# Latent attention in a two-layer block: gate pieces in two halves around the turned weights, and another order of their reading

## The chip, the cores and the metric

The kernel runs on one core of a Trainium2 chip. The metric is device time in microseconds (us) of one launch, median of three runs. Engines are named as in the profile: PE is TensorE (PEld its weight loads), DVE is VectorE, ACT is ScalarE, POOL is GpSimd, SP is SyncE.

## The reference

512 tokens pass a first block (sparse and dilated attention, then a mixture of experts) and two further layers. The change lies in the attention routine that both parts share. The two stages that matter:

```
# first block: three attentions over 8 heads, mixed by gates
o = gb[..., 0:1] * o_c + gb[..., 1:2] * o_s + gb[..., 2:3] * o_w
gm = jax.nn.sigmoid(mg)                       # merge gates, 16 pieces of 128 rows
# each of the two further layers: latent attention over 8 heads
sc = jnp.einsum('bqhd,bkhd->bhqk', q_blk, k) * scale
sc = jnp.where(qpos[:, None] >= kpos[None, :], sc, jnp.finfo(jnp.float32).min)
p = jax.nn.softmax(sc, axis=-1)
o = jnp.einsum('bhqk,bkhe->bqhe', p, v)
gates = jax.nn.sigmoid(gate_logits)           # (h @ w_in), 24 pieces of 128 rows
```

## The kernel before

`paired_attention` (L202) does all three attention stages. Work goes in **units**: one pair of heads (sides u = 0, 1) and one block of 128 queries. The latent stage (`mla`, called once in each of the two layers) has 16 units: four pairs of heads times t = 0 to 3, where unit n has t = n mod 4 and sees (t + 1) x 128 keys. The stage `nsa` of the first block has 16 units too, `dil` has 8. The order on each engine is written out by hand, and semaphores alone join the engines.

The steps of a unit, by the names of the code:

- `score(n)` on PE (L259, masks L263): products of queries and keys into PSUM.
- `largest(n)` on DVE (L337, L338), `exps(n)` on ACT (L394).
- `weigh(n)`: the weights of side 0 are scaled on DVE (L348, L359); in `mla` those of side 1 are scaled on ACT (L414).
- `turn(n, c)` on PE (L278): transposes of the weights, in chunks of up to two key blocks (one chunk for t = 0 and 1, two for t = 2 and 3). `copy(n, c)` (L368) brings a chunk from PSUM to SBUF, in `mla` always on DVE.
- `mix(n, c)` on PE (L294): value products from the copied chunk. `store(n)` on ACT (L408).

`AHEAD` is the number of score buffers: 2 in `mla`, 1 in `nsa` and `dil`. Beside the attention PE computes **gate pieces**: 24 matmuls of 128x512 each (`Gates.tensor`, L2800 to L2802 through `three`). In `mla` 11 of the 16 units have one, those in `GATE_PAIRS` = (0, 1, 2, 3, 5, 7, 9, 11, 13, 14, 15), called gated below; units 4, 6, 8, 10 and 12 have none. In `nsa` every unit has one. All gate pieces of these stages go through a single PSUM bank: the first matmul of the next piece waits until DVE has read the last one (`take`, L1269). The split of a later weight piece into two parts (`high` on ACT L562, `low` on DVE L570) goes along with each gated unit, and SP loads the pieces ahead.

The order before, for unit n of `mla`: PE does the last `mix` of unit n - 1, the whole gate piece, `score(n + 2)`, then waits for the scaled weights, and does `turn` with the next `mix` right behind it. DVE does `weigh(n)`, `largest(n + 1)`, `low`, the copies, `take(n)`. ACT does its part of `weigh(n)`, `store(n - 1)`, `exps(n + 1)`, `high`. With `lead` true (`mla` and `nsa`) the first gate piece stands ahead of the loop.

Of the kernel before, what the change touches and what calls it, by code (L numbers as in the profile page):

```python
# [26 lines left out]
P = 128  # L27
# [3 lines left out]
DC = D // P  # L31
# [170 lines left out]
def paired_attention(nc, name, C, pairs, scale, cols, places, beside, by_scalar, lead):  # L202
# [4 lines left out]
    N, SIDES, WIDE, RING = len(pairs), 2, 4 * P, 3  # L207
# [4 lines left out]
    AHEAD = len(scores_at)  # L212
    two_engines = AHEAD == 2
    with Stage(nc, name) as st:
# [25 lines left out]
        with st.block() as block:  # L240
# [9 lines left out]
            @block.tensor  # L250
            def _(pe):
                def score(n):
                    scores = scores_at[n % AHEAD]
                    if n >= AHEAD:
                        pe.wait_ge(exp_done, SIDES * (n - AHEAD + 1))
                    for bank, parts, width in pairs[n].products:
                        for j, (q, keys) in enumerate(parts):
                            for u in range(SIDES):
                                nc.tensor.matmul(scores[:, u, bank:bank + width], q[u], keys[u], start=(j == 0), stop=False)  # L259
                        for after, at, mask in pairs[n].masks:  # L260
                            if after == bank:
                                for u in range(SIDES):
                                    mm = nc.tensor.matmul(scores[:, u, at:at + mask.shape[1]], C.mask_ident, mask, start=False, stop=True)  # L263
                    mm.then_inc(scored, 1)

                def turn(n, c):
                    g = before[n] + c
                    if g >= 2:
                        pe.wait_ge(*copied_after(g - 2))
                    if c < extra:  # L270
                        of = pairs[n].extra[0]
                        mm = nc.tensor.transpose(turned[g % 2][0:of.shape[1], 0:P], of, C.ident[:, :])
                    else:
                        blocks = blocks_of(n, c)
                        for u in range(SIDES):
                            for j, (col, _) in enumerate(blocks):
                                at = (u * len(blocks) + j) * P
                                mm = nc.tensor.transpose(turned[g % 2][:, at:at + P], probs[n % 2][:, u, col:col + P], C.ident[:, :])  # L278
                    mm.then_inc(turn_done, 1)

                def mix(n, c):
                    g = before[n] + c
                    pe.wait_ge(*copied_after(g))
                    if c == 0 and n >= 1:
                        pe.wait_ge(stored, n)
                    if c < extra:
                        v = pairs[n].extra[1]
                        mm = nc.tensor.matmul(mixed, v, probs_t[g % RING][0:v.shape[0], 0:P], start=True, stop=False)
                    else:
                        blocks = blocks_of(n, c)  # L290
                        for j, (_, v) in enumerate(blocks):
                            for u in range(SIDES):
                                rows, at = slice(64 * u, 64 * u + 64), (u * len(blocks) + j) * P
                                mm = nc.tensor.matmul(mixed[rows, :], v[:, rows], probs_t[g % RING][:, at:at + P],  # L294
                                                      start=(c == 0 and j == 0), stop=(c == chunks[n] - 1 and j == len(blocks) - 1))
                    mm.then_inc(chunk_mixed, 1)

                for n in range(AHEAD):
                    score(n)
                if lead:  # L300
                    beside.tensor(pe, 0)
                else:
                    idle_products(nc, C, turned[0], 10)
                for n in range(N):
                    if AHEAD == 1 and n + 1 < N:
                        score(n + 1)
                    if n >= 1:
                        mix(n - 1, chunks[n - 1] - 1)
                    if n >= 1 or not lead:
                        beside.tensor(pe, n)  # L310
                    if AHEAD == 2 and n + 2 < N:
                        score(n + 2)
                    for c in range(chunks[n]):
                        if c == extra:
                            pe.wait_ge(scaled, by_vector * (n + 1))
                            if two_engines:
                                pe.wait_ge(scaled_s, n + 1)
                        turn(n, c)
                        if c >= 1:
                            mix(n, c - 1)  # L320
                mix(N - 1, chunks[N - 1] - 1)
                idle_products(nc, C, turned[0], 8)

            @block.vector
            def _(dve):
# [14 lines left out]
                def weigh(n):  # L340
                    if n >= 2:
                        dve.wait_ge(scaled, by_vector * (n - 1))
                        if two_engines:
                            dve.wait_ge(scaled_s, n - 1)
                    for u in range(SIDES):
                        at = SIDES * n + u + 1
                        dve.wait_ge(exp_done, at)
                        V.reciprocal(rden[n % 2][:, u, :], den[n % 2][:, u, :]).then_inc(inverted, 1)  # L348
                        if u >= by_vector:
                            continue  # L350
                        dve.wait_ge(inverted, at)
                        if weighted:
                            V.tensor_tensor(wgt[n % 2][:, u, :], rden[n % 2][:, u, :], pairs[n].weights[:, u, :],
                                            ALU.mult).then_inc(weights_done, 1)
                            dve.wait_ge(weights_done, at)
                        by = wgt[n % 2]
                        for k, (col, width) in enumerate(pairs[n].parts):
                            pr = probs[n % 2][:, u, col:col + width]
                            ins = V.tensor_scalar(pr, pr, by[:, u, k:k + 1], None, ALU.mult)  # L359
                        ins.then_inc(scaled, 1)  # L360
# [9 lines left out]
                largest(0)  # L370
                for n in range(N):
                    weigh(n)
                    if AHEAD == 1:
                        beside.vector(dve, n)
                    if n + 1 < N:
                        largest(n + 1)
                    if AHEAD == 2:
                        beside.vector(dve, n)
                    for c in range(by_scalar, chunks[n]):
                        copy(n, c)  # L380
                    beside.after(dve, n)

            @block.scalar
            def _(act):
# [55 lines left out]
class CompressedWeights:  # L440
# [24 lines left out]
    def tensor(self, pe, n):  # L465
        if n not in self.FIRST:
            return
        h = self.FIRST.index(n)
        if h >= 1:
            pe.wait_ge(self.shift_done, h)  # L470
        for j in range(2):
            for t in range(TT):
                at = (TT * j + t) * 2 * N_CMP
                out = self.bank[:, at:at + 2 * N_CMP].rearrange("p (u c) -> p u c", u=2)
                self.nc.tensor.matmul(out, self.z[:, Z_Q + 2 * h + j, t * P:(t + 1) * P], self.k_both, start=True, stop=False)
                add = self.masks[:, t * N_CMP:(t + 1) * N_CMP].unsqueeze(1).to_broadcast([P, 2, N_CMP])
                mm = self.nc.tensor.matmul(out, self.ident, add, start=False, stop=True)
        mm.then_inc(self.scored, 1)
# [700 lines left out]
class Angles:  # L1179
# [42 lines left out]
    def turn(self, act, j):  # L1222
        act.wait_ge(self.reduced, j + 1)
        to = (self.C.sin2, self.C.cos2)[j]
        self.nc.scalar.activation(to[self.rows, :], self.left[j][self.rows, :], ACT.Sin)


class Gates:
# [40 lines left out]
        self.nc.vector.tensor_tensor(self.m[:, s, :], self.place(c)[0], self.x_rstd,  # L1269
                                     ALU.mult).then_inc(self.taken, 1)  # L1270

    def tensor(self, pe, c):
        bank, last = self.place(c)
        if last >= 0:
            pe.wait_ge(self.taken, last + 1)
        hi, lo = self.stream.ready(pe, self.at(c))
        for k, at in enumerate(slices(DC)):
            mm = three(self.nc, bank, hi[:, at], lo[:, at], self.x_hi[:, k, :], self.x_lo[:, k, :], k == 0,
                       k == DC - 1)
        mm.then_inc(self.stream.used, 1)  # L1280


class GatesByUnit:
# [39 lines left out]
class GatesByPair(GatesByUnit):  # L1323
# [9 lines left out]
    def after(self, dve, n):  # L1333
        if n in self.slots:
            self.gates.take(dve, self.slots[n])


def pool_and_gla(nc, name, C, y, values, w_a2, w_pool, scale, m, head_root, bank, gates):
# [1473 lines left out]
def slices(n, width=P):  # L2812
    return [slice(k * width, (k + 1) * width) for k in range(n)]
# [777 lines left out]
```

## Time and profile before

| | us |
|---|---|
| median of 3 runs | 3619.53 |
| lowest, highest | 3617.75, 3620.05 |
| span of the profiled execution | 3620.0 |
| PE busy in it | 3509.2 (97%) |
| DVE busy | 2323.1 (64%) |
| ACT busy | 1428.6 (39%) |

The profile is of one execution. A row of a timeline begins with the start and the duration in us; what stands in square brackets is the idle time of that engine just before, and what ended it. The end of a PE matmul is modelled, so the idle time of PE is a little shorter than what the next instruction has waited, and the idle time of its weight loads (PEld) is also shown. PEclk is the granted TensorE clock: 1.00 is 2.4 GHz, 0.50 is 1.2 GHz.

### The profile page before, as it was taken

The page shows a single profiled execution, that of the slowest core. Times are in us where ns is not written, and L with a number is a line of the kernel's source. Part 1 is how long each engine was busy: PE and PEld are TensorE (multiplying, and loading weights), DVE is VectorE, ACT ScalarE, POOL GpSimd, SP SyncE. Part 2 cuts the span into 40 slices and gives each one's busy share as a digit, 9 for nine tenths or more (in the row PEclk, how much of TensorE's full clock was granted, in tenths as well). Part 3 has the DMA queues.
Part 4 walks back from the last instruction along what each step waited for, and adds up shares of the span by engine and source line. Part 5 has one row for each costly group of instructions (what it writes and reads, how often), then busy time and mean ns, then how long its engine had stood idle before and what let it go on. Part 6 is the DMA issues. An engine that isn't in the chain of part 4 may idle for free. (4 is left out here: it accounts for less than half of the span.)

```text
span 3620.0 us, 47480 instructions
## 1 busy us (share of the span) xinstructions
PE 3509.2 (97%) x18217; PEld 2997.8 (83%) x18224; DVE 2323.1 (64%) x4211; ACT 1428.6 (39%) x2390; POOL 377.4 (10%) x280
## 2 busy tenths in 40 slices
PE   8999999999999899999999999999999999999998
PEld 6776778999999899999887767788878776778887
DVE  6656766889999798888635546544343544655433
ACT  4343343433899443333323234433232323443221
POOL 1000000000233336434100000000000000000000
PEclk9999999999999999999999999999999999999999
DMA  4321243555899999999522224232322222423332
GB/s 148 102 65 50 65 142 100 202 168 168 306 364 367 370 367 396 388 377 389 204 94 82 77 70 152 79 107 97 93 88 93 82 75 73 145 85 105 99 92 71
DMA packets 213172, 597.38 MB, mean 165 GB/s; under 512 B 22258, under 2 KB 80404, under 8 KB 211412
## 3 DMA queue, kind: packets, MB, share of 16 engines
q1 hardware_dynamic: 176084, 460.13, 38.1%
q0 software_dynamic: 36864, 134.23, 9.6%
q8 instruction: 145, 2.38, 0.3%
q14 instruction: 79, 0.65, 0.1%
HBM read 523.36 MB, written 69.21 MB: 164 GB/s over the span
## 5 line engine op out<-in xcount | busy, mean ns | idle before, releaser
L562 ACT ACTIVATE stream_hi<-stream_raw 128x1024 fp32r<-128x1024 f32 (+1 forms) x611 | 638.9, 1046 | 1060.3 <-PE ffn_ps L2802 416.9
L570 DVE TENSOR_TENSOR stream_lo<-stream_raw,stream_hi 128x1024 fp32r<-128x1024 f32 (+1 forms) x611 | 740.3, 1212 | 442.2 <-ACT stream_hi L562 439.6
L1140 PE MATMUL experts_ps<-mix_a_hi,stream_hi 128*128 128x384 f32 x1024 | 342.9, 335 | 15.4 <-issue 15.4
L598 PE MATMUL experts_ps<-h_hi,stream_hi 128*128 128x384 f32 x1024 | 346.7, 339 | 1.1 <-PEq L728 1.1
L1140 PE MATMUL experts_ps<-mix_a_lo,stream_hi 128*128 128x384 f32 x1024 | 342.8, 335 | 0.0
L1140 PE MATMUL experts_ps<-mix_a_hi,stream_lo 128*128 128x384 f32 x1024 | 342.7, 335 | 0.0
L598 PE MATMUL experts_ps<-h_lo,stream_hi 128*128 128x384 f32 x1024 | 342.2, 334 | 0.0
L598 PE MATMUL experts_ps<-h_hi,stream_lo 128*128 128x384 f32 x1024 | 342.2, 334 | 0.0
L2800 PE MATMUL mid_ps<-h_hi,stream_hi 128*128 128x512 f32 x672 | 280.3, 417 | 4.1 <-PEq L3030 2.2
L2800 PE MATMUL ffn_ps<-h_hi,stream_hi 128*128 128x512 f32 x704 | 280.7, 399 | 2.7 <-DVE h_lo L2856 2.7
L2802 PE MATMUL ffn_ps<-h_hi,stream_lo 128*128 128x512 f32 x704 | 274.0, 389 | 0.0
L2801 PE MATMUL ffn_ps<-h_lo,stream_hi 128*128 128x512 f32 x704 | 274.0, 389 | 0.0
L2801 PE MATMUL mid_ps<-h_lo,stream_hi 128*128 128x512 f32 x672 | 264.8, 394 | 0.0
L2802 PE MATMUL mid_ps<-h_hi,stream_lo 128*128 128x512 f32 x672 | 264.4, 393 | 0.0
L662 POOL DMA_INDIRECT experts_rows<-u_rows,experts_slot_at x128 | 160.4, 1253 | 622.9 <-DVE experts_rows L672 476.3
L662 POOL DMA_INDIRECT experts_rows<-v,experts_slot_at x128 | 195.7, 1529 | 217.8 <-DVE mix_sums L690 188.7
L1140 PEld LDWEIGHTS experts_ps<-mix_a_hi,stream_hi 128*128 128x128 f32 x1024 | 192.8, 188 | 15.7 <-issue 15.7
L598 PEld LDWEIGHTS experts_ps<-h_hi,stream_hi 128*128 128x128 f32 x1024 | 192.4, 188 | 1.8 <-issue 1.4
L1140 PEld LDWEIGHTS experts_ps<-mix_a_lo,stream_hi 128*128 128x128 f32 x1024 | 192.8, 188 | 0.0
L1140 PEld LDWEIGHTS experts_ps<-mix_a_hi,stream_lo 128*128 128x128 f32 x1024 | 192.8, 188 | 0.0
L598 PEld LDWEIGHTS experts_ps<-h_lo,stream_hi 128*128 128x128 f32 x1024 | 192.5, 188 | 0.0
L598 PEld LDWEIGHTS experts_ps<-h_hi,stream_lo 128*128 128x128 f32 x1024 | 192.2, 188 | 0.0
(510 smaller groups left out, 6840.3 us busy)
## 6 DMA issues: line engine op xcount, KB each, us to landing
stream_raw<-u SPq DMA_DIRECT2D x128, 512.0 KB, 3.9
stream_raw<-v SPq DMA_DIRECT2D x128, 512.0 KB, 8.2
stream_raw<-l_gu SPq DMA_DIRECT2D x88, 512.0 KB, 3.3
expert_hidden<-experts_gelu SPq DMA_DIRECT2D x128, 192.0 KB, 4.1
expert_weights<-built SPq DMA_DIRECT2D x12, 2048.0 KB, 10.6
built<-expert_weights SPq DMA_DIRECT2D x16, 1536.0 KB, 13.9
stream_raw<-l_gate SPq DMA_DIRECT2D x48, 512.0 KB, 3.9
built<-expert_hidden SPq DMA_DIRECT2D x124, 192.0 KB, 8.7
```

The lines of the kernel that those rows point to most:

```text
L562: self.nc.scalar.activation(self.hi[n % self.RING][:, 0:w], self.raw[n % self.RAW][:, 0:w], ACT.Copy).then_inc(self.hi_done, 1)
L570: self.nc.vector.tensor_tensor(self.lo[n % self.RING][:, 0:w], self.raw[n % self.RAW][:, 0:w], self.hi[n % self.RING][:, 0:w].bitcast(F32) ...
L598: mm = self.nc.tensor.matmul(self.ps[n % 2], a, b[:, k, :], start=(k == 0 and m == 0), stop=(k == DC - 1 and m == 2))
L662: self.nc.gpsimd.indirect_dma_start(self.rows[n % self.RING][:, :], None, source, bass.IndirectOffsetOnAxis(ap=self.at[:, j:j + 1], axis=0 ...
L1140: mm = nc.tensor.matmul(out[d][:, DIRECT:SEQ], v, a[b % RING][:, :], start=(b == 0 and m == 0), stop=(b == KEYS - 1 and m == 2))
L2800: nc.tensor.matmul(out, hi, x_hi, start=first, stop=False)
L2801: nc.tensor.matmul(out, hi, x_lo, start=False, stop=False)
L2802: return nc.tensor.matmul(out, lo, x_hi, start=False, stop=last)
```

## The change

In `mla` (`AHEAD` 2) PE has another order. For a gated unit: `score(n + 2)`, first half of the gate piece (12 matmuls), the wait for the scaled weights, all of `turn(n)`, second half of the gate piece, all of `mix(n)`. For a unit without a gate piece: the wait, `turn(n)`, `score(n + 2)`, `mix(n)`. Unit 0 is gated but has its `score(2)` behind `turn(0)`. On DVE `take(n - 1)` moves from behind the copies of unit n - 1 to behind `weigh(n)`, in front of `largest(n + 1)`. ACT, SP and POOL keep their order.

For `AHEAD` 1 the order stays, with one difference: the gate piece that `lead` had put ahead of the loop now stands in the loop, so that in `nsa` it comes behind `score(1)`.

```
                 for n in range(AHEAD):
                     score(n)
-                if lead:
-                    beside.tensor(pe, 0)
-                else:
+                if not lead:
                     idle_products(nc, C, turned[0], 10)
                 for n in range(N):
-                    if AHEAD == 1 and n + 1 < N:
-                        score(n + 1)
-                    if n >= 1:
-                        mix(n - 1, chunks[n - 1] - 1)
-                    if n >= 1 or not lead:
+                    if AHEAD == 1:
+                        if n + 1 < N:
+                            score(n + 1)
+                        if n >= 1:
+                            mix(n - 1, chunks[n - 1] - 1)
                         beside.tensor(pe, n)
-                    if AHEAD == 2 and n + 2 < N:
+                        for c in range(chunks[n]):
+                            if c == extra:
+                                scaled_by_both(n)
+                            turn(n, c)
+                            if c >= 1:
+                                mix(n, c - 1)
+                        continue
+                    gated = n in beside.slots
+                    if gated and n >= 1 and n + 2 < N:
                         score(n + 2)
+                    beside.half(pe, n, 0)
+                    scaled_by_both(n)
                     for c in range(chunks[n]):
                         turn(n, c)
-                        if c >= 1:
-                            mix(n, c - 1)
-                mix(N - 1, chunks[N - 1] - 1)
+                    if (not gated or n == 0) and n + 2 < N:
+                        score(n + 2)
+                    beside.half(pe, n, 1)
+                    for c in range(chunks[n]):
+                        mix(n, c)
+                if AHEAD == 1:
+                    mix(N - 1, chunks[N - 1] - 1)
...
                     weigh(n)
+                    if AHEAD == 2 and n >= 1:
+                        beside.after(dve, n - 1)
...
-                    beside.after(dve, n)
+                    if AHEAD == 1:
+                        beside.after(dve, n)
+                if AHEAD == 2:
+                    beside.after(dve, N - 1)
...
-    def tensor(self, pe, c):
+    def tensor(self, pe, c, rows=range(DC)):
         bank, last = self.place(c)
-        if last >= 0:
+        if rows[0] == 0 and last >= 0:
             pe.wait_ge(self.taken, last + 1)
...
+    def half(self, pe, n, which):
+        if n in self.slots:
+            self.gates.tensor(pe, self.slots[n], range(which * DC // 2, (which + 1) * DC // 2))
```

PE, first `mla` stage, around the turned weights of unit 1 (a gated one; `stream_const,mla_probs` is `turn`, `mla_probs_t,v` is `mix`, `k,q` and `stream_masks` are `score`, `h_hi` and `h_lo` the gate piece). Before:

```order
L2802 MATMUL mid_ps<-h_hi,stream_lo 128x512
L259 MATMUL mid_ps<-k,q 128x512 x4
L263 MATMUL mid_ps<-stream_masks 128x128 x2
L278 MATMUL mid_ps<-stream_const,mla_probs 128x128 x4
L294 MATMUL mid_ps<-mla_probs_t,v 64x128 x4
L2800 MATMUL mid_ps<-h_hi,stream_hi 128x512
```

`mix` stood right behind `turn`, and the gate piece behind `mix`. Now the turned weights of unit 3 (the line numbers of the gate piece are 24 higher in the changed file):

```order
L2826 MATMUL mid_ps<-h_hi,stream_lo 128x512
L2824 MATMUL mid_ps<-h_hi,stream_hi 128x512
L2825 MATMUL mid_ps<-h_lo,stream_hi 128x512
L2826 MATMUL mid_ps<-h_hi,stream_lo 128x512
L278 MATMUL mid_ps<-stream_const,mla_probs 128x128 x8
L2824 MATMUL mid_ps<-h_hi,stream_hi 128x512
L2825 MATMUL mid_ps<-h_lo,stream_hi 128x512
L2826 MATMUL mid_ps<-h_hi,stream_lo 128x512
```

`turn` has gate matmuls on both sides; `mix` has moved behind twelve of them.

The same engine at unit 4, which has no gate piece, before:

```order
L259 MATMUL mid_ps<-k,q 128x384 x4
L263 MATMUL mid_ps<-stream_masks 128x128 x2
L278 MATMUL mid_ps<-stream_const,mla_probs 128x128 x2
L294 MATMUL mid_ps<-mla_probs_t,v 64x128 x2
L2800 MATMUL mid_ps<-h_hi,stream_hi 128x512
```

And now:

```order
L278 MATMUL mid_ps<-stream_const,mla_probs 128x128 x2
L259 MATMUL mid_ps<-k,q 128x384 x4
L263 MATMUL mid_ps<-stream_masks 128x128 x2
L294 MATMUL mid_ps<-mla_probs_t,v 64x128 x2
L259 MATMUL mid_ps<-k,q 128x512 x4
L263 MATMUL mid_ps<-stream_masks 128x128 x2
L2824 MATMUL mid_ps<-h_hi,stream_hi 128x512
```

The score products of unit 6 have moved between `turn` and `mix` of unit 4, those of unit 7 ahead of the gate piece of unit 5.

PE at the start of `nsa`, before:

```order
L250 UNCONDITIONAL_BRANCH
L259 MATMUL first_ps<-z 128x128 x4
L263 MATMUL first_ps<-masks_sb 128x128 x4
L2800 MATMUL first_ps<-h_hi,stream_hi 128x512
L2801 MATMUL first_ps<-h_lo,stream_hi 128x512
```

And now:

```order
L250 UNCONDITIONAL_BRANCH
L259 MATMUL first_ps<-z 128x128 x4
L263 MATMUL first_ps<-masks_sb 128x128 x4
L259 MATMUL first_ps<-z 128x256 x4
L263 MATMUL first_ps<-masks_sb 128x128 x4
L2824 MATMUL first_ps<-h_hi,stream_hi 128x512
L2825 MATMUL first_ps<-h_lo,stream_hi 128x512
```

The score products of unit 1, which wait for the exponentials of unit 0, have moved ahead of the first gate piece.

## Rows read from the trace of the kernel before

**Rows 1.** The page: busy time of each engine, with its share of the span.

```profile
PE 3509.2 (97%) x18217; PEld 2997.8 (83%) x18224; DVE 2323.1 (64%) x4211; ACT 1428.6 (39%) x2390; POOL 377.4 (10%) x280
```

**Rows 2.** Waits of PE, whole run: line, releaser, total us, times, longest us.

```profile
PE mid_ps L294 <- DVE mla_probs_t L368: 18.0, 32, 0.8
...
PE up_ps L2800 <- DVE up_y_lo L2664: 1.9, 1, 1.9
...
PE mid_ps L278 <- issue: 0.7, 4, 0.2
```

**Rows 3.** Busy time in the two `mla` stages: us and count by engine, PEclk, DMA.

```profile
2085.00:2207.00 122.00, 112.35 (x667) 76.89 (x668) 60.42 (x159) 41.64 (x108) 0.00 (x0) 1.00 0.26 74
2991.00:3113.00 122.00, 111.96 (x666) 76.59 (x664) 60.33 (x159) 41.38 (x107) 0.00 (x0) 1.00 0.27 76
```

**Rows 4.** Who waited for the copied chunks, by tile: total us, times.

```profile
  PEld mid_ps L294: 27.0, 40
```

**Rows 5.** Timeline of the first `mla` stage: weight loads behind `turn`, and one hand-over.

```profile
2105.75 0.42 PEld L294 LDWEIGHTS mid_ps<-mla_probs_t,v 128*64 128x64 f32 x8 [1.02 <-DVE mla_probs_t L368]
...
2114.38 0.64 PEld L294 LDWEIGHTS mid_ps<-mla_probs_t,v 128*64 128x64 f32 x12 [0.80 <-DVE mla_probs_t L368]
...
2149.95 0.42 PEld L294 LDWEIGHTS mid_ps<-mla_probs_t,v 128*64 128x64 f32 x8 [0.58 <-DVE mla_probs_t L368]
...
2153.85 0.20 PEld L294 LDWEIGHTS mid_ps<-mla_probs_t,v 128*64 128x64 f32 x4 [0.75 <-DVE mla_probs_t L368]
...
2164.13 0.72 PEld L259 LDWEIGHTS mid_ps<-k,q 64*128 64x128 f32 x8 [0.17 <-issue]
```

**Rows 6.** Timeline of the same stage, DVE and ACT, from the copy of unit 1.

```profile
2105.01 0.69 DVE L368 COPY mla_probs_t<-mid_ps 128x512 f32<-128x512 f32 x1 [3.87 <-PE mid_ps L278]
2105.62 0.68 DVE L1269 TENSOR_TENSOR m_rows<-mid_ps,x_rstd 128x512 f32<-128x512 f32 x1
...
2106.22 0.15 DVE L348 RECIPROCAL mla_rden<-mla_den 128x1 f32<-128x1 f32 x1
...
2106.82 0.67 DVE L337 TENSOR_REDUCE mla_top<-mid_ps 128x1 f32<-128x512 f32 x1
...
2108.50 0.69 ACT L394 ACTIVATE mla_probs<-mid_ps,mla_bias 128x512 f32<-128x512 f32 x1
...
2109.17 1.05 ACT L562 ACTIVATE stream_hi<-stream_raw 128x1024 fp32r<-128x1024 f32 x1
2110.26 1.23 DVE L570 TENSOR_TENSOR stream_lo<-stream_raw,stream_hi 128x1024 fp32r<-128x1024 f32 x1 [1.79 <-ACT stream_hi L562]
```

**Rows 7.** Timeline of the same stage, PE: a gate piece's start, scores, `mix`.

```profile
2096.45 0.50 PE L2800 MATMUL mid_ps<-h_hi,stream_hi 128*128 128x512 f32 x1 [0.16 <-DVE m_rows L1269]
...
2102.12 2.19 PE L259 MATMUL mid_ps<-k,q 64*128 64x512 f32 x8
...
2105.76 0.66 PE L294 MATMUL mid_ps<-mla_probs_t,v 128*64 128x128 f32 x8 [0.78 <-DVE mla_probs_t L368]
...
2164.13 0.91 PE L259 MATMUL mid_ps<-k,q 64*128 64x128 f32 x8
```

**Rows 8.** Timeline of the start of `nsa`, PE and ACT.

```profile
297.54 0.40 PE L263 MATMUL first_ps<-masks_sb 128*128 128x128 bf16 x4
...
299.93 0.22 ACT L394 ACTIVATION_READ_ACCUMULATOR nsa_probs<-first_ps,nsa_bias 128x1 f32 x1
...
303.39 1.13 PE L259 MATMUL first_ps<-z 64*128 64x256 f32 x8
...
306.82 0.48 PE L288 MATMUL first_ps<-nsa_probs_t,v_cmp 64*128 64x128 f32 x2 [1.42 <-DVE nsa_probs_t L368]
...
307.81 2.93 PE L259 MATMUL first_ps<-z 64*128 64x384 f32 x8 [0.50 <-ACT nsa_probs L394]
```

**Rows 9.** PE in two stretches: busy us (count), PEclk, DMA share, GB/s.

```profile
474.00:478.00 4.00, 4.00 (x12) 0.59 1.03 353
...
1997.00:2007.00 10.00, 10.00 (x29) 0.50 0.17 59
```

More of the change, by code:

```diff
@@ L296, in mix, with scaled_by_both @@
                     mm.then_inc(chunk_mixed, 1)
+                def scaled_by_both(n):
+                    pe.wait_ge(scaled, by_vector * (n + 1))
+                    if two_engines:
+                        pe.wait_ge(scaled_s, n + 1)
                 for n in range(AHEAD):
                     score(n)
-                if lead:
-                    beside.tensor(pe, 0)
-                else:
+                if not lead:
                     idle_products(nc, C, turned[0], 10)
                 for n in range(N):
-                    if AHEAD == 1 and n + 1 < N:
-                        score(n + 1)
-                    if n >= 1:
-                        mix(n - 1, chunks[n - 1] - 1)
-                    if n >= 1 or not lead:
-                        beside.tensor(pe, n)
-                    if AHEAD == 2 and n + 2 < N:
+                    if AHEAD == 1:
[3 more added lines that the diff above has]
+                            mix(n - 1, chunks[n - 1] - 1)
+                        beside.tensor(pe, n)
+                        for c in range(chunks[n]):
[7 more added lines that the diff above has]
+                    if gated and n >= 1 and n + 2 < N:
@@ L312, in _ @@
                         score(n + 2)
+                    beside.half(pe, n, 0)
+                    scaled_by_both(n)
                     for c in range(chunks[n]):
[L314 to L317, printed above, removed]
                         turn(n, c)
-                        if c >= 1:
-                            mix(n, c - 1)
-                mix(N - 1, chunks[N - 1] - 1)
+                    if (not gated or n == 0) and n + 2 < N:
+                        score(n + 2)
@@ L1270, in take @@
                                      ALU.mult).then_inc(self.taken, 1)
-    def tensor(self, pe, c):
+    def tensor(self, pe, c, rows=range(DC)):
         bank, last = self.place(c)
-        if last >= 0:
+        if rows[0] == 0 and last >= 0:
             pe.wait_ge(self.taken, last + 1)
         hi, lo = self.stream.ready(pe, self.at(c))
-        for k, at in enumerate(slices(DC)):
+        for k in rows:
+            at = slice(k * P, (k + 1) * P)
             mm = three(self.nc, bank, hi[:, at], lo[:, at], self.x_hi[:, k, :], self.x_lo[:, k, :], k == 0,
                        k == DC - 1)
-        mm.then_inc(self.stream.used, 1)
+        if rows[-1] == DC - 1:
+            mm.then_inc(self.stream.used, 1)
 class GatesByUnit:
```

## Prediction

> **What bounds the kernel now.** I read the page first. PE is busy 3509.2 of 3620.0 us [rows 1]: it is the bound, 111 us of idle time are all that an edit which only reorders can win, and an engine other than PE matters only where PE waits for it. So the second view is the list of PE's waits. Its longest line belongs to this stage: `mix` waits 32 times, 18.0 us, for the copy of the turned weights [rows 2]. 32 is every unit of both latent stages. The third view is the busy time in the stages: 112.35 and 111.96 of 122 us [rows 3], so some 10 us of idle time in each, nearly all of it this wait, and a granted clock of 1.00 throughout. DVE (60 us of 122) and ACT (42) have room on average; whether they have it at the right place is the question below.
>
> **What the wait is worth.** The 18.0 us are counted from the modelled end of the last transpose. The weight loads show the same wait from the side that is issued: 27.0 us, 40 times [rows 4]. By kind of unit it is 0.75 us (t = 0), 1.02 (t = 1), 0.80 (t = 2) and 0.58 (t = 3) [rows 5]. Each kind comes 8 times: 8 x 3.15 = 25.2 us; the other eight times are second chunks, (27.0 - 25.2) / 8 = 0.2 each. Not all of that is lost: where nothing is waited for, the load behind narrow products still comes 0.17 us late (the last of [rows 5]), and the 0.2 are just that. So a unit can win 0.58, 0.85, 0.63, 0.41, and all of them 25.2 - 32 x 0.17 = 19.8 us.
>
> **Part 1, gated units (22).** Between `turn` and `mix` now stand 12 gate matmuls. A whole piece takes from 2096.45 to 2102.12, 5.67 us [rows 7], a half 2.8. The copies take 0.61 us for one chunk of 512 (2105.01 to 2105.62) and twice that for two [rows 6]: 1.2 plus some 0.1 to start, under the cover of 2.8. The wait goes. If the cover were gone it would be back at its 0.41 to 0.85. The split adds one more change from narrow products to a gate piece, and takes one away (`mix` to gate becomes `mix` to `score`); I cost it at nothing, with 0 to 0.1 us x 22 = 2 us for the range.
>
> **Part 2, units without a gate piece (10).** Between `turn` and `mix` stands `score(n + 2)`. For n = 4, 8, 12 it is 384 keys wide, near 1.8 us (between the 0.91 of 128 and the 2.19 of 512 [rows 7]): cover enough. For n = 6 and 10 it is the narrow one, 0.91 and its mask, 0.97 in all, and here the move on DVE counts. Call T the end of `turn(9)`. DVE copies to T + 0.7, weighs (0.60 from 2106.22 to 2106.82 [rows 6]), then stands in front of `take(9)` until the second half piece is done at T + 2.8, and reads it in 0.6 (2105.62 to 2106.22): T + 3.5. `largest(11)` is 512 wide, 1.7 us (2106.82 to the second exponential at 2108.50 [rows 6]): T + 5.2. Only then the first copy, to T + 5.8. PE: half piece 2.8, `mix(9)` 0.6 [rows 7], `turn(10)` 0.9, score 1.0: T + 5.3. A wait of about 0.6 with the signal's way stays at units 6 and 10 of both layers, 0.7 as I take it: 4 x 0.7 = 2.8 us. Units 14 and 15 have no score left: `take` ends at T + 3.5, and the next gate piece would start at T + 2.8 + 0.6 (unit 14) or + 0.8 (unit 15). I take 0.8 us in both layers together.
>
> **Part 3, what else waits behind the moved `take`.** On DVE `largest`, `low` and the copies are queued behind it; on ACT `exps`, then `high`, for which `low` waits. From the end of a half piece the chain is: `take` 0.7, from `largest` to the second exponential 1.7, that one and `high` to 2110.26, 1.8, `low` 1.2, copy 0.6 [rows 6]: 6.0 us. PE has for it, until `mix(n)` needs the copy: `mix` 0.6, a score of 1 to 2.2, half piece 2.8, `turn` 0.6, half piece 2.8: at least 7.8. It is hidden, with 1.8 us to spare; without that it would cost PE its excess in each gated unit. SP stores a piece behind its `take`, some 3 us later than before, and a load is queued behind the store; the loads run pieces ahead of a unit of about 9 us, and I cost that at nothing. The waits that PE had apart from the copies (0.7 us in front of `turn` in 4 units [rows 2]; 0.16 for the bank of the gate pieces [rows 7], once a layer) make 1.0 us in all, and go.
>
> **Part 4, the start of `nsa`.** The diff moves a gate piece there as well. Before, it covered the exponentials of unit 0. Now PE ends `score(0)` at 297.94 and must wait for the last of them, 299.93 + 0.22 = 300.15 [rows 8]: 2.2 us idle where there was none. Behind it the two waits of 1.42 and 0.50 [rows 8] go, since the gate piece now covers weighing and `largest(1)`. Idle time alone: 2.2 - 1.9 = 0.3 us lost, but the 8 score matmuls at 307.81 took 2.93 us [rows 8] where 384 keys take about 1.8: the clock was low there. In the other place where PE sat idle that long, 1.9 us in front of the up product [rows 2], the next 4 us had a clock of 0.59 [rows 9], worth 4 x 0.41 = 1.6 us. So one low stretch goes (307.8 to about 311) and one comes (from about 301, in the gate piece). Counted through by instruction, `score(1)` 1.5, gate piece 5.7, transposes 0.7, from 300.2 with 1.7 us for the low clock: `score(2)` starts at 309.9 and ends at 311.7, where it ended at 311.07 before. I take +0.9 us; without the low stretch it is -0.8.
>
> The Trainium skill (TensorE: Matmul & The Clock Gate, "Why this matters for your kernels") warns only of gaps longer than this one; by it the low stretch would not come and the sum would be 1.7 us smaller. The trace has 1.9 us of idle time followed by a clock of 0.59, and the measurement decides. The same page ("A second HAM failure mode: psum-queue depth-cycling") says that many short idles between groups of products can themselves bring the clock down; the stage here has 32 such gaps at a clock of 1.00 [rows 3], so nothing is won back there.
>
> **Sum.** -19.8 - 1.0 + 2.8 + 0.8 + 0.9 = -16.3 us. 3620.0 - 16.3 = 3603.7 for the profiled execution; that is 0.5 above the median of the runs (3619.53), so 3603 for the median.
>
> **Rivals.**
> (a) *DVE has less room than I count.* If the 0.7 us wait also comes at units 4, 8 and 12 and half the gated units keep some 0.4, then 6 x 0.7 + 11 x 0.4 = 8.6 us stay: a gain of 8, 3611. For it: `take` now waits for PE, with everything else of DVE and ACT behind it. Against it: 1.8 us to spare.
> (b) *Slower.* The ring half piece, `take`, `largest`, `exps`, `high`, `low`, copy, `mix` becomes the bound of all 22 gated units. It decides once it is over the time that PE has, 7.8 to 9 us against the 6.0 of the rows. To eat the gain of 16.3 and lose 0.2% (7 us) beyond it, it would need 24 / 22 = 1.1 us over that in each, some 9 to 10 us in all, one and a half times its rows. At that: 3627.
> (c) *The clock.* Low stretches occur with PE fully busy too: 1997 to 2007 at 0.50 [rows 9], 5 us lost, and the like in the second layer. What I move is upstream of them; if one goes, 3598, if one more comes, 3608.
> (d) *Everything hidden*: no new waits and no low stretch in `nsa`: -19.8 - 1.0 - 0.8 = -22, 3598.
> (e) *It doesn't do what it says*: PE would find another wait of the same size in place of each, since `mix` and the next `turn` hang on the same DVE. Then 3620. The trace has DVE idle 3.87 us in front of the copy [rows 6], which speaks against it.
>
> **How the numbers follow.** Forecast (gain of 13 to 20) 0.60; (d) 0.12; (c) 0.10, half to each side; (a) 0.12; (e) 0.03; (b) 0.03. 0.2%, about what a measurement of this kernel can tell from no change, is 7.2 us: faster means below 3612.3. That holds for the forecast, (c), (d) and most of (a): 0.91; same 0.06; slower 0.03. The range: 3596 (all hidden and a low stretch less) to 3612 (rival (a)); what lies outside is (b), (e), a part of (a) and of (d).
>
> **What would show it.** Right: the wait of `mix` for the copies falls from 18.0 us to under 3; the `mla` stages take some 8.6 us less each; the rest of that wait stands at units 6 and 10; one wait of 2.2 us for `nsa_probs` at 298, and a low clock near 301 instead of 308. Wrong: PE waiting for ACT or DVE in front of `score` or `turn` in gated units (part 3, rival (b)); a gate piece waiting for its bank in many units; low stretches of the clock in other places.

## The result

| | before | changed |
|---|---|---|
| median of 4 runs on the same chip, us | 3618.66 | 3600.85 |
| lowest, highest | 3617.75, 3620.05 | 3596.70, 3602.54 |
| ratio, 95% interval | | 0.9949 [0.9937, 0.9961] |
| span of the profiled execution | 3620.0 | 3594.9 |

The kernel is 17.8 us faster, 16.5 were forecast for the median (3603). Its profiled execution is the fastest of its four and stands 25.1 us below that of before, so the two numbers have to be explained apart.

The list of PE's waits of the changed kernel (line, releaser, total us, times, longest us) answers to [rows 2]:

```profile
PE first_ps L259 <- ACT nsa_probs L412: 2.3, 1, 2.3
...
PE mid_ps L294 <- DVE mla_probs_t L381: 2.1, 4, 0.5
PE up_ps L2824 <- DVE up_y_lo L2688: 1.9, 1, 1.9
...
PE mid_ps L2824 <- DVE m_rows L1287: 0.4, 2, 0.2
```

`mix` waits 4 times instead of 32, 2.1 us instead of 18.0. The waits of 1.42 and 0.50 us at the start of `nsa` [rows 8] are gone, and 2.3 us for the exponentials have come in their place. The wait in front of `turn` (L278, 0.7 us) is gone from the list.

How long a latent stage takes is read from its first score product to the first idle product behind its last `mix`. Timeline of PE, before:

```profile
2085.05 0.91 PE L259 MATMUL mid_ps<-k,q 64*128 64x128 f32 x8 [0.44 <-PEq L1615]
...
2206.41 0.82 PE L2809 MATMUL mid_ps<-stream_masks 128*128 128x512 bf16 x3
```

and changed:

```profile
2084.52 0.91 PE L259 MATMUL mid_ps<-k,q 64*128 64x128 f32 x8 [0.44 <-PEq L1639]
...
2195.47 1.90 PE L2833 MATMUL mid_ps<-stream_masks 128*128 128x512 bf16 x8
```

That is 121.4 us before and 111.0 us now; the second layer has 121.3 and 110.9. **The two stages give 20.8 us.** The start of `nsa`, from its first score to the first value product of unit 0 (L294), took 14.2 us and takes 12.8. The remaining 2.9 us of the 25.1 (20.8 in the stages, 1.4 at the start of `nsa`) lie in code that the change doesn't touch, nearly all between the two latent stages (2206.41 to 2991.84 before, 2195.47 to 2978.03 now: 785.4 and 782.6 us). There the clock differs (PE busy us, count, PEclk, DMA share, GB/s; first before, then changed):

```profile
2870.00:2950.00 80.00, 75.38 (x333) 0.89 0.22 68
```

```profile
2870.00:2950.00 80.00, 78.06 (x339) 0.94 0.25 69
```

0.05 of 80 us is up to 4 us of full clock; 2.8 us is what the two stretches differ by. Which executions get it changes from run to run: another profiled execution of the same changed kernel (e5 below) has 0.89 there, and 785.5 us between the stages.

### The profile page after: what moved, and what is told of

It is laid out like the page before. It is cut to its first block and busy times, and to the rows that moved or that the text cites. A ratio compares the mean times of both kernels' runs of the same rounds, so it can differ in the third digit from the quotient of the medians.

```text
span 3594.9 us, 47480 instructions
## 1 busy us (share of the span) xinstructions
PE 3500.2 (97%) x18217; PEld 2993.1 (83%) x18224; DVE 2325.5 (65%) x4211; ACT 1430.5 (40%) x2390; POOL 352.1 (10%) x280
## 5 line engine op out<-in xcount | busy, mean ns | idle before, releaser
L680 POOL DMA_INDIRECT experts_rows<-v,experts_slot_at x128 | 169.4, 1324 | 243.8 <-DVE mix_sums L708 214.0
```

Source lines behind the costliest of these rows:

```text
L680: self.nc.gpsimd.indirect_dma_start(self.rows[n % self.RING][:, :], None, source, bass.IndirectOffsetOnAxis(ap=self.at[:, j:j + 1], axis=0 ...
```

## The experiments

Each kernel was run beside the kernel before on the same chip. The stage lengths and the `nsa` stretch are read from each trace as above.

| kernel | stage 1, us | stage 2, us | `nsa` start, us | median, us | before, us | ratio, 95% interval |
|---|---|---|---|---|---|---|
| before | 121.4 | 121.3 | 14.2 | | | |
| change | 111.0 | 110.9 | 12.8 | 3600.85 | 3618.66 | 0.9949 [0.9937, 0.9961] |
| e5 change again | 111.0 | 110.9 | 14.4 | 3598.90 | 3620.04 | 0.9942 [0.9929, 0.9956] |
| e1 latent stages only | 110.9 | 110.9 | 12.7 | 3597.75 | 3621.84 | 0.9939 [0.9926, 0.9953] |
| e2 `nsa` only | 121.3 | 121.3 | 14.4 | 3620.84 | 3621.84 | 1.0001 [0.9992, 1.001] |
| e3 take behind copies | 115.1 | 115.1 | 14.4 | 3607.66 | 3621.84 | 0.9964 [0.9952, 0.9976] |
| e4 score ahead of turn | 112.2 | 112.3 | 14.4 | 3603.63 | 3621.84 | 0.9956 [0.9941, 0.9971] |
| e6 piece not split | 110.7 | 113.8 | 14.4 | 3601.35 | 3620.04 | 0.9949 [0.9934, 0.9964] |
| e10 one more DVE step | 115.4 | 112.3 | 14.4 | 3605.82 | 3618.52 | 0.9968 [0.9955, 0.9981] |
| e7 three more DVE steps | 124.2 | 121.2 | 14.4 | 3622.82 | 3620.04 | 1.0009 [1.0, 1.0018] |
| e8 other pairs, `nsa` halves | 109.7 | 109.8 | 10.6 | 3593.23 | 3620.04 | 0.9923 [0.9909, 0.9936] |
| e9 the same, one split | 108.6 | 108.6 | 10.6 | 3589.72 | 3618.52 | 0.9921 [0.9908, 0.9935] |

### The two halves of the change apart

e1 has the changed latent stages, and `nsa` as before:

```
                 if not lead:
                     idle_products(nc, C, turned[0], 10)
+                elif AHEAD == 1:
+                    beside.tensor(pe, 0)
...
-                        beside.tensor(pe, n)
+                        if n >= 1 or not lead:
+                            beside.tensor(pe, n)
```

> The changed order in the two latent stages alone; the start of the nsa stage is as before (gate piece 0 ahead of score(1)). Theory: all of the gain is the copy waits that go, so each latent stage takes 111.0 us from its first score product to its last idle one's start (121.4 before), 20.8 us less in both, and the kernel is 20 us faster than before, give or take 2 us of low clock elsewhere. Rival (the prediction's part 4): the nsa part costs 0.9 us, so that this kernel is 0.9 us faster than the full change; against it the trace of the changed kernel, by which the nsa part saves 1.4 us and this one would be that much slower.

e2 is the kernel before with the new start of `nsa`:

```
-                if lead:
+                if lead and AHEAD == 2:
                     beside.tensor(pe, 0)
-                else:
+                elif not lead:
                     idle_products(nc, C, turned[0], 10)
...
-                    if n >= 1 or not lead:
+                    if n >= 1 or not lead or AHEAD == 1:
```

> Only the start of the nsa stage is changed (score(1) ahead of gate piece 0); the latent stages are as before. Prediction's part 4: PE waits 2.2 us for the exponentials, a low stretch of the clock follows near 301 and the one near 308 goes, +0.9 us from the first score of nsa to gate piece 1. Rival, by the trace of the changed kernel: no low stretch follows 2.3 us of idle time, -1.4 us over the same span. The latent stages stay at 121.4 us and the wait of mix for the copies at 18.0 us. In the total either is at the edge of what 5 rounds can tell.

e1 alone is 24.1 us faster, 2 us more than its expectation allowed; e2 alone cannot be told from the kernel before. All of the gain that the change brings is in the latent stages. What e1 shows beyond 20.8 lies elsewhere in its profiled execution: 1.5 us at the start of `nsa`, which had no low stretch of the clock this time, and 1.3 between the stages (784.1 us). e2 keeps its wait of 18.0 us, e1 has 2.1.

The length of the `nsa` start depends on the clock, and both theories had half of it. PE in four stretches of e2 (busy us, count, PEclk, DMA share, GB/s):

```profile
296.00:300.00 4.00, 1.97 (x17) 1.00 0.00 0
300.00:304.00 4.00, 3.35 (x16) 0.66 0.10 14
304.00:308.00 4.00, 4.00 (x18) 0.91 0.32 119
308.00:312.00 4.00, 4.00 (x29) 1.00 0.02 4
```

and of e1, which has the old start:

```profile
304.00:308.00 4.00, 2.08 (x19) 1.00 0.28 105
308.00:312.00 4.00, 4.00 (x28) 1.00 0.00 0
```

In e2 the clock falls behind the 2.3 us of idle time, as it does in e3 to e7 and e10; in the one profiled execution of the change that was compared first it did not. In e1 the two waits of 1.4 and 0.5 us are followed by a full clock, where the kernel before had a low stretch. So the new order takes 12.8 us without a low stretch and 14.4 with it, the old one 12.7 and 14.2. **Like with like, the `nsa` part costs 0.1 to 0.2 us.**

> The full change once more, beside the kernels of this call. Theory: 111.0 us for each latent stage, 14.4 us from the first score of nsa to the first value product of its unit 0 where a low stretch of the clock follows the 2.3 us of idle time, 12.8 where it doesn't; in the total 20 to 24 us faster than before. If the total again shows 18 us while the stages show 20.8, the rest is lost to low stretches of the clock elsewhere.

The second run of the change, on another chip, is 21.1 us faster than before, with the same stages to 0.1 us. The two intervals overlap; the stages account for 20.8.

### What on DVE and PE makes the gain

e3 leaves `take` where it was, behind the copies:

```
-                    if AHEAD == 2 and n >= 1:
-                        beside.after(dve, n - 1)
...
-                    if AHEAD == 1:
-                        beside.after(dve, n)
-                if AHEAD == 2:
-                    beside.after(dve, N - 1)
+                    beside.after(dve, n)
```

> The new order on PE, but DVE reads the gate piece where it did before, behind the copies and ahead of the next weighing. Theory: DVE then stands in front of the second half piece (2.8 us) before it weighs the next unit, so that PE waits for the scaled weights in the units without a gate piece: about 0.6 us at units 4, 8, 12 and 1.5 us at 6 and 10, in place of 0.5 at the mix of 6 and 10: each latent stage 3 to 4 us longer than with the change (114 to 115 us), the total 7 us slower than it. Rival: the place of this step does not matter since DVE is busy for half of the stage only; then 111 us and the same total.

The stages are 4.1 us longer than with the change. Its waits of PE in the latent stages are this one line:

```profile
PE mid_ps L278 <- DVE mla_probs L372: 10.2, 10, 1.5
```

Ten times, once for each unit without a gate piece, and the wait is now in front of `turn`. In the timeline of its second stage the units 4 and 6 show it as 0.7 and 1.5 us:

```profile
3024.70 0.41 PE L278 MATMUL mid_ps<-stream_const,mla_probs 128*128 128x128 f32 x2 [0.70 <-DVE mla_probs L372]
...
3037.81 0.85 PE L278 MATMUL mid_ps<-stream_const,mla_probs 128*128 128x128 f32 x6 [1.49 <-DVE mla_probs L372]
```

DVE stands in front of the second half piece before it weighs. The move of `take` is a needed part of the change: the PE order alone gives 12.5 of the 20.8 us. The other half, `take` moved in the kernel before with PE's order left alone, was not run.

e4 keeps the score products ahead of `turn` in the units without a gate piece:

```
+                    if not gated and n + 2 < N:
+                        score(n + 2)
                     beside.half(pe, n, 0)
...
-                    if (not gated or n == 0) and n + 2 < N:
+                    if n == 0:
                         score(n + 2)
```

> As the change, but in the five units without a gate piece score(n+2) stays ahead of turn, so that mix stands right behind turn there. Theory: those units keep their wait for the copy, 0.6 us at 4, 8, 12 and 0.7 to 0.8 at 6 and 10, the others have none: each stage about 2 us longer than with the change (113 us), the total 4 us slower. Rival: the score is no cover, since DVE has take and largest ahead of the copies; then 111 us.

```profile
PE mid_ps L294 <- DVE mla_probs_t L383: 5.7, 10, 0.7
```

The wait for the copy stands in all ten of those units, 5.7 us where the change has 2.1 in four of them, and the stages are 1.3 us longer (2 expected). Keeping the score ahead of `turn` costs 2.6 of the 20.8 us, an eighth of the whole.

e6 doesn't split the gate piece. Unit 0 then has nothing to cover its weighing:

```
-                    beside.half(pe, n, 0)
                     scaled_by_both(n)
...
-                    beside.half(pe, n, 1)
+                    beside.tensor(pe, n)
```

> The gate piece is not split: all 24 of its matmuls stand between turn and mix. Theory: the cover of the copy is what counts, not the split; the only new wait is at unit 0, where nothing covers the first weighing (about 1.2 us per stage), so each stage is 112 us and the total 2 us slower than with the change. Rival: the first half is needed to cover the weighing in every gated unit; then PE waits in front of turn by some 0.5 to 1 us in 11 units, each stage 5 to 10 us longer (116 to 121 us).

The first stage takes 110.7 us, less than with the split and less than the 112 expected, although PE waits 0.7 us at unit 0. The theory that the cover of the copy is what counts holds; the rival, by which every gated unit needs the first half, falls. The second stage took 113.8, and there the clock was low right behind that wait (the same wait in the first stage was followed by 1.00):

```profile
2975.00:2982.00 7.00, 6.30 (x33) 0.77 0.08 29
2982.00:2986.00 4.00, 4.00 (x12) 0.55 0.66 197
```

### How much room DVE has

e7 and e10 put k = 3 and k = 1 more DVE instructions, whose results are not used, behind `take`:

```
                     if AHEAD == 2 and n >= 1:
                         beside.after(dve, n - 1)
+                        for _ in range(k if n - 1 in beside.slots else 0):
+                            V.tensor_tensor(beside.spare[_][:, :], beside.gates.x_rstd, beside.gates.x_rstd, ALU.mult)
```

> As the change, with three more DVE instructions of 128x512 (0.6 to 0.7 us each, their results are not used) behind take in each of the 11 gated units of each stage: 2 us more on the chain take, largest, exps, high, low, copy, mix. Prediction's part 3: 1.8 us to spare there, so almost nothing in gated units and up to 2 us more at the mix of units 6 and 10: each stage 4 to 5 us longer (115 to 116). Rival (DVE has less room): by a count of every unit's rows, some 1 us more is lost at units 4, 8, 12 and 14 as well, 8 us per stage (119), and the total 16 us slower than with the change.

> As e7, with one more DVE instruction of 128x512 behind take in place of three. Theory (DVE has less room than the prediction counted only at units 6 and 10): the copy of units 6 and 10 comes 0.6 us later, 1.1 us of wait in place of 0.5, the others stay without a wait: each stage 1.3 us longer than with the change (112.3 us), the total 3 us slower, and no low stretch of the clock inside the stages. Rival: the gated units are at their limit too, 0.6 us more in each, 6 us per stage (117).

The waits of PE for the copies, first e7, then e10:

```profile
PE mid_ps L296 <- DVE mla_probs_t L383: 14.5, 12, 2.3
```

```profile
PE mid_ps L296 <- DVE mla_probs_t L383: 4.5, 4, 1.1
```

With 0.6 us more (e10) only units 6 and 10 wait, 1.1 us instead of 0.5, and the undisturbed stage is 112.3 us, as expected. With 1.9 us more (e7) the timeline of PE shows units 4 and 6 so:

```profile
3035.59 0.44 PE L296 MATMUL mid_ps<-mla_probs_t,v 128*64 128x128 f32 x4 [0.68 <-DVE mla_probs_t L383]
...
3049.15 0.88 PE L296 MATMUL mid_ps<-mla_probs_t,v 128*64 128x128 f32 x12 [2.33 <-DVE mla_probs_t L383]
```

Units 8 and 12 wait 0.7 as well, unit 10 2.3, unit 14 0.6, and unit 15 waits 0.7 for its bank; the other gated units still don't wait. The rival of e7's expectation was right on where, and 7.2 us of waits for copies per stage stand against 1.1 with the change. The queue of DVE in a unit without a gate piece, with all that stands ahead of its copy, is this (DVE, e7, unit 6):

```profile
3044.40 0.69 DVE L1291 TENSOR_TENSOR m_rows<-mid_ps,x_rstd 128x512 f32<-128x512 f32 x1 [1.48 <-PE mid_ps L2830]
3045.01 1.89 DVE L391 TENSOR_TENSOR mla_spare<-x_rstd 128x512 f32<-128x512 f32 x3
3046.81 0.69 DVE L352 TENSOR_REDUCE mla_top<-mid_ps 128x1 f32<-128x512 f32 x1
...
3048.40 1.02 DVE L383 COPY mla_probs_t<-mid_ps 128x512 f32<-128x512 f32 x2
```

What no theory had is the clock; e10's said that no low stretch would come inside the stages. The stages of e7 took 124.2 and 121.2 us where the waits alone give some 118, and one stage of e10 took 115.4 instead of 112.3. PE behind one wait of each, in e10 and in e7 (busy us, count, PEclk):

```profile
2156.00:2160.00 4.00, 4.00 (x23) 0.51 0.00 0
```

```profile
3075.00:3079.00 4.00, 3.52 (x20) 0.54 0.02 4
```

The other wait of the same 1.1 us in the same stage of e10 was followed by a full clock. In all, the low stretch came behind one of the four waits of 1.1 us (e10) and behind three of the four of 2.3 us (e7), and cost about 3 us each time.

### Two further versions

The rows of the change name what it left: 0.5 us at units 6 and 10, where the score is the narrow one, and 2.3 us at the start of `nsa`. e8 changes both:

```
-GATE_PAIRS = (0, 1, 2, 3, 5, 7, 9, 11, 13, 14, 15)
+GATE_PAIRS = (0, 1, 2, 3, 6, 7, 10, 11, 13, 14, 15)
...
                     if AHEAD == 1:
+                        if n == 0 and lead:
+                            beside.half(pe, 0, 0)
                         if n + 1 < N:
                             score(n + 1)
                         if n >= 1:
                             mix(n - 1, chunks[n - 1] - 1)
-                        beside.tensor(pe, n)
+                        if n == 0 and lead:
+                            beside.half(pe, 0, 1)
+                        else:
+                            beside.tensor(pe, n)
```

> As the change, with two more edits. GATE_PAIRS leaves out units 4, 5, 8, 9, 12 in place of 4, 6, 8, 10, 12, so that units with a narrow score(n+2) have a gate piece; and in nsa the first gate piece stands in two halves around score(1). Theory: the waits for the copy at units 6 and 10 (2.1 us in all) go, 0.2 us of waits for the scaled weights come at 5 and 9: each stage 110.0 to 110.3 us. In nsa the first half covers the exponentials of unit 0 and the second the weighing and largest(1): the wait of 2.3 us goes, and with it the low stretch of the clock, 10.5 us in place of 12.8 or 14.4. In the total 4 us faster than the change. Rival: in unit 5 or 9 PE waits for the scaled weights behind a unit without a gate piece by as much as it saves; then the stages stay at 111.

The stages are 109.7 us, 1.2 less, and no wait for copies or weights is left in them. At the start of `nsa` neither the wait nor a low stretch is left. Timeline of PE in e8:

```profile
300.66 1.14 PE L259 MATMUL first_ps<-z 64*128 64x256 f32 x8
...
307.44 0.66 PE L294 MATMUL first_ps<-nsa_probs_t,v_tok 128*64 128x128 f32 x8
```

e9 also leaves the gate piece whole in all units but unit 0:

```
-                    beside.half(pe, n, 0)
+                    if n == 0:
+                        beside.half(pe, 0, 0)
...
-                    beside.half(pe, n, 1)
+                    if n == 0:
+                        beside.half(pe, 0, 1)
+                    else:
+                        beside.tensor(pe, n)
```

> The kernel of e8 with the gate piece split in unit 0 of each latent stage alone; in all other units all 24 matmuls stand between turn and mix. Theory: e6 had 110.67 us in its first stage with a new wait of 0.7 us at unit 0, so 0.9 us less than the change apart from that wait, from fewer changes between kinds of products; with unit 0 split again the wait doesn't come: 108.7 to 109.1 us per stage (109.75 in e8), the total 1 to 2 us faster than e8. Rival: the shorter stage of e6 came from something else, and the wait for weighing shows up behind the units without a gate piece; then 109.8 or more.

108.6 us per stage: another 1.1 us, with 108.7 to 109.1 expected. PE is busy without a gap in both (the stretches lie inside the stages):

```profile
2077.00:2184.00 107.00, 106.88 (x648) 1.00 0.28 82
2972.00:3079.00 107.00, 106.88 (x652) 1.00 0.28 82
```

e8 and e9 are 26.8 and 28.8 us faster than the kernel before on their chips, the fastest kernels of this study. Of the two, the stages tell them apart (2.3 us in both stages together), the intervals of the totals don't.

## Why the prediction was right

**The wait (part 1) was read rightly, and its worth was set too low.** The forecast took 17.2 us from the two stages (19.8 + 1.0 less 3.6 of new waits); they gave 20.8, 10.4 in each where 8.6 had been named as the sign. The rows tell where. PE's time in the stages can be split by kind of product, each group counted from the start of its first product to the start of the next group's first, so that a wait falls to the group in front of it (us, both stages together; differences before rounding):

| group | before | changed | difference |
|---|---|---|---|
| transposes (`turn`) | 41.0 | 17.4 | -23.5 |
| value products (`mix`) | 24.6 | 22.9 | -1.6 |
| gate pieces | 124.4 | 127.3 | +2.9 |
| scores with their masks | 52.7 | 54.2 | +1.5 |
| sum | 242.7 | 221.9 | -20.8 |

Three terms of the sum were off, and not all in one direction.

The first is the 0.17 us that was subtracted 32 times, 5.4 us, as a hand-over that stays. The transposes alone lose 23.5 us, where the forecast allowed 19.8 for all waits behind them; it is nearer to the 25.2 that the weight loads had waited, with nothing taken off. Timeline of PE around the turned weights of unit 2, before:

```profile
2112.99 0.82 PE L278 MATMUL mid_ps<-stream_const,mla_probs 128*128 128x128 f32 x6
...
2114.38 0.88 PE L294 MATMUL mid_ps<-mla_probs_t,v 128*64 128x128 f32 x12 [0.56 <-DVE mla_probs_t L368]
2115.31 0.50 PE L2800 MATMUL mid_ps<-h_hi,stream_hi 128*128 128x512 f32 x1
```

and changed:

```profile
2105.07 0.47 PE L2824 MATMUL mid_ps<-h_hi,stream_hi 128*128 128x512 f32 x1
...
2107.93 0.82 PE L278 MATMUL mid_ps<-stream_const,mla_probs 128*128 128x128 f32 x6
2108.50 0.48 PE L2824 MATMUL mid_ps<-h_hi,stream_hi 128*128 128x512 f32 x1
...
2111.41 0.88 PE L294 MATMUL mid_ps<-mla_probs_t,v 128*64 128x128 f32 x12
2112.21 1.33 PE L259 MATMUL mid_ps<-k,q 64*128 64x256 f32 x8
```

The rows are to be read from start to start. Six transposes took 1.39 us until `mix` started, and take 0.57 until the gate matmul behind them starts: 0.82 less, where the forecast allowed 0.63 for such a unit. The row that showed 0.17 [rows 5] was one of a score behind narrow products. A gate matmul behind transposes isn't delayed like that. Where a score follows them, it is slower. Timeline of PE, unit 6 of the changed kernel, six transposes behind a `mix` and ahead of a score, 0.80 us:

```profile
2132.76 0.88 PE L278 MATMUL mid_ps<-stream_const,mla_probs 128*128 128x128 f32 x6
2133.56 0.91 PE L259 MATMUL mid_ps<-k,q 64*128 64x128 f32 x8
```

The second is the split, which the sum had at nothing (0 to 2 us in its range). In unit 2 the halves take 2.86 and 2.91 us, together 0.1 more than the 5.67 of a whole piece [rows 7]; over the 22 pieces the gate matmuls take 2.9 us longer. With its effects on the neighbours a split costs 0.11 us by e9 against e8 (2.3 us for 20), 2.5 for 22. It hides half of the first error.

The third is the new waits (part 2, part 3): 3.6 us forecast, 2.1 + 0.4 by the modelled ends. The place was right, units 6 and 10 in both layers, with 0.5 us each by the modelled ends (about 0.6 by the starts) where 0.7 stood. Timeline of PE, unit 6 of the changed kernel:

```profile
2135.21 0.88 PE L294 MATMUL mid_ps<-mla_probs_t,v 128*64 128x128 f32 x12 [0.52 <-DVE mla_probs_t L381]
```

The 0.8 us for the bank at units 14 and 15 were 0.4, at unit 14 alone:

```profile
2180.62 0.50 PE L2824 MATMUL mid_ps<-h_hi,stream_hi 128*128 128x512 f32 x1 [0.20 <-DVE m_rows L1287]
```

What is left of the 3.6 us, near 1 us, lies in the small waits that went. The forecast had 1.0 us for them, of which 0.3 stood for the bank of the gate pieces, read from the idle time of the matmuls [rows 7]. The weight loads show more (waits of PEld before: total us, times, longest us):

```profile
PEld mid_ps L2800 <- DVE m_rows L1269: 2.7, 10, 0.4
```

In unit 2 above it is why the 12 value products took 0.93 us until the gate piece behind them, and now take 0.80. What each of these small waits was worth isn't separated further.

That the median came within 2.2 us of the forecast 3603 is in part luck. The stages gave 3.6 us more than the sum had, and runs of one kernel scatter by as much: 17.8 us in the first comparison, 21.1 in e5.

**Part 3, the room behind `take`,** is borne out for the gated units ahead of others: 1.9 us more on DVE (e7) brings no wait in them but at unit 14, which has no score behind it, and the part had 1.8 to spare. It is not borne out as the room of the stage: the units without a gate piece have less, and rival (a) named the right units (4, 8, 12) and the right queue. e7 shows how near the slower side was. With 1.9 us more on DVE in each gated unit the whole gain is gone, where rival (b) asked for some 3 to 4. The two stages lose 23.5 us against the change, of which 13.8 are waits (14.5 + 1.8 less 2.1 + 0.4, by the modelled ends); nearly all of the rest goes with three low stretches of the clock behind them, 3 us each.

**Part 4, `nsa`, had the right waits and the wrong sum.** 2.2 us of new wait were forecast and 2.3 came; the 1.4 and 0.5 went. The low stretch does come behind it in most executions. But its +0.9 doesn't follow from its own count, by which `score(2)` ends at 311.7 instead of 311.07, 0.6 us later. That count added up single durations; the same stretch by trace takes 0.2 us more than before (e2, with the low stretch in both). That is the mis-sized term: 0.9 instead of 0.2. Of the profiled executions with this 2.3 us gap (the change twice, e2 to e4, e6, e7, e10), all but one have the low stretch. The Trainium skill (TensorE: Matmul & The Clock Gate, "Why this matters for your kernels") warns only of longer gaps; one execution agrees with it, seven do not.

**Rival (c)** came in the profiles: low stretches of the clock outside the latent stages make the 25.1 us of the two profiles out of the 20.8 of the stages, 1.4 of it at the start of `nsa` and 2.9 far from the change. That they also make the 17.8 us of the medians is likely but not shown, since only one execution of each has a trace. **Rivals (d) and (e)** fall: waits stay at the places named, and nothing of the size of the old ones came in their place.

## What to carry to other kernels

When one engine is the bound and waits after each of its own results for another engine to copy it, part of its independent work belongs between the result and its use; a split is needed only where something else in front of it needs cover too. Then look at the queue of the copying engine: what waits for the covering work (here `take`) must stand behind what the bound engine waits for next, and the place with the least cover, not the average busy share, sets how much room is left. Wherever little independent work is left over, give it to the units whose own cover is shortest.

## What the runs showed of the hardware

Gaps of 1.1 us on PE were followed by a clock of 0.51 for 4 us in one case and by a full clock in the other three (e10). Behind the gaps of 2.3 us in the latent stages of e7 the clock fell three times of four; in its second stage it was 0.54 behind one and 1.00 behind the other. The 32 gaps of 0.4 to 0.8 us of the kernel before had 1.00 throughout [rows 3], but a single one of 0.7 us at the start of a stage was followed by 0.55 over 4 us in one layer and by 1.00 in the other (e6). Removing a gap can be worth more than its length, and one profile doesn't show by how much.

Twelve matmuls of 128x512 between transposes and value products take 2.9 us, and 24 in one row 5.7: each piece that is split costs about 0.1 us. Six transposes take 0.57 us until a gate matmul behind them starts, and 0.80 behind a `mix` and ahead of a score.
